# First norm of a fused two-block transformer kernel: how its sum of squares, the vector c and the constants come on chip

## What is computed

```python
c_act = jax.nn.silu(c)                       # c: (1, 1024)
mod = c_act @ w_ada[l] + b_ada[l]            # w_ada: 1024 x 6144
sh1, sc1, g1, sh2, sc2, g2 = jnp.split(mod, 6, axis=-1)
xn = modulate(rmsnorm(h, norm1_g[l]), sh1, sc1)
p = xn @ w_in[l]
...
def rmsnorm(x, g):
    y = x * lax.rsqrt(jnp.mean(x * x, axis=-1, keepdims=True) + EPS)
    return y * g
def modulate(xn, shift, scale):
    return xn * (1.0 + scale) + shift
```

## Time and profile before

| | |
|---|---|
| Median of three runs | 3202.27 us |
| The profiled execution, its own time | 3200.54 us |
| Its span in the profile | 3198.7 us (1.84 less) |
| TensorE (PE) busy | 3165.5 us, 99% of the span |
| VectorE (DVE) busy | 1867.6 us, 58% |
| ScalarE (ACT) busy | 532.1 us, 17% |
| First TensorE record | 4.00 us |
| TensorE enters the loop over k | 20.44 us |

### The profile page before, as it was taken

One profiled execution on the slowest core, in us unless ns is written; L12 is line 12 of the kernel. 1 busy time (PEld: TensorE's weight loads), 2 busy tenths in 40 slices (PEclk: granted clock), 3 DMA queues, 4 the chain that ended last, 5 costly groups with the idle time before them and its releaser, 6 DMA issues.

```text
span 3198.7 us, 36062 instructions
## 1 busy us (share of the span) xinstructions
PE 3165.5 (99%) x14174; PEld 2575.5 (81%) x14174; DVE 1867.6 (58%) x3244; ACT 532.1 (17%) x1120; POOL 240.8 (8%) x218
## 2 busy tenths in 40 slices
PE   9999999999999999999999999999999999999999
PEld 3888758888888888885488888888888854788887
DVE  6356845764347764465676664466644656766643
ACT  2111122000111000115621000110001157210001
POOL 1244410000000000003000000000000030000000
PEclk9999999999999999999999999999999999999999
DMA  5254321222222222223012222222222230122221
GB/s 239 81 183 147 143 79 53 93 79 93 85 90 82 90 89 86 89 74 119 7 66 79 93 84 91 90 79 93 86 89 89 74 119 7 61 85 93 79 84 61
DMA packets 43881, 288.28 MB, mean 90 GB/s; under 512 B 5405, under 2 KB 5405, under 8 KB 12737
## 3 DMA queue, kind: packets, MB, share of 16 engines
q1 hardware_dynamic: 39024, 271.14, 23.9%
q0 software_dynamic: 4688, 14.85, 1.4%
HBM read 281.76 MB, written 2.11 MB: 89 GB/s over the span
## 4 chain that ended last, share of the span: by engine, by line
PE 93%; DVE 4%; ACT 1%; DVEq 1%; issue 1%; DMA 0%; POOL 0%; ACTq 0%
PE ps L872 77%; PE ps L574 3%; PE ps L1283 2%; PE ps L1316 2%; PE ps L1009 2%; PE ps L1228 1%; PE ps L1297 1%; DVE arena L1953 1%; PE ps L555 1%; PE ps L899 1%; PE ps L1255 0%; PE ps L1248 0%; ACT arena L1640 0%; PE ps L956 0%; PE ps L969 0%
## 5 line engine op out<-in xcount | busy, mean ns | idle before, releaser
L872 PE MATMUL ps<-arena 128*128 128x256 f32 x5456 | 1244.9, 379 | 0.1
L872 PEld LDWEIGHTS ps<-arena 128*128 128x128 f32 x5456 | 1037.5, 190 | 140.6 <-DVE arena L2126 0.5
L872 PE MATMUL ps<-arena,ring 128*128 128x256 f32 x2768 | 646.0, 379 | 0.5 <-ACT arena L1368 0.5
L872 PEld LDWEIGHTS ps<-arena,ring 128*128 128x128 f32 x2768 | 526.0, 190 | 71.6 <-ACT arena L1368 0.9
L872 PE MATMUL ps<-xn,ring 128*128 128x256 f32 x2272 | 518.9, 379 | 5.6 <-DVE arena L1769 2.1
L872 PEld LDWEIGHTS ps<-xn,ring 128*128 128x128 f32 x2272 | 431.5, 190 | 71.4 <-issue 9.3
L1763 DVE TENSOR_TENSOR arena<-arena,ps 128x512 f32<-128x512 f32 x173 | 118.9, 687 | 545.1 <-PE ps L872 487.8
L1736 DVE TENSOR_TENSOR arena<-ring 128x512 f32<-128x512 f32 (+1 forms) x194 | 131.1, 676 | 347.9 <-PE ps L872 347.8
L872 PE MATMUL ps<-xn,arena 128*128 128x256 f32 x1264 | 302.2, 379 | 0.0
L872 PEld LDWEIGHTS ps<-xn,arena 128*128 128x128 f32 x1264 | 240.4, 190 | 32.4
L1556 ACT ACTIVATE arena<-arena 128x512 f32<-128x512 f32 x88 | 55.4, 630 | 883.6 <-DVE arena L2245 883.6
(11 more groups left out here) (327 smaller groups left out, 2510.2 us busy)
## 6 DMA issues: line engine op xcount, KB each, us to landing
ring<-in_w_up_a SPq DMA_DIRECT2D x44, 1024.0 KB, 4.8
ring<-in_w_up_b SPq DMA_DIRECT2D x44, 1024.0 KB, 4.8
ring<-in_w_ff SPq DMA_DIRECT2D x32, 1024.0 KB, 4.8
ring<-in_w_ada SPq DMA_DIRECT2D x24, 1024.0 KB, 4.9
ring<-in_w_down_a SPq DMA_DIRECT2D x16, 1024.0 KB, 4.8
ring<-in_w_down_b SPq DMA_DIRECT2D x16, 1024.0 KB, 4.8
ring<-in_w_in SPq DMA_DIRECT2D x14, 1024.0 KB, 4.8
ring<-in_w_out SPq DMA_DIRECT2D x12, 1024.0 KB, 5.6
```

The costliest lines, as they stand in the source:

```text
L872: mm = nc.tensor.matmul(out_ap, w, operand(product, quads[i]), start=at not in opened, stop=last_chunk and i == len(quads) - 1, skip_group ...
```

## The change

It has five parts.

- The constants are no longer loaded first. `ones` becomes the last of the five matrices and is written on chip by a VectorE memset; the other four are loaded ahead of the third chunk of `w_v`. TensorE's filler product reads the ones four times over in place of four constants, and there are two such products ahead of the squares, not three.
- c is loaded as one row in one partition (`c_one`). ScalarE applies Silu to that row before its squares; TensorE spreads it over all partitions by two products with a row of ones; ScalarE copies one half of the result out of PSUM and VectorE the other.
- VectorE adds squares before TensorE sees them: tiles 0 to 3 become one, and tile 7 is added to tile 5.
- TensorE multiplies four arrays by ones: the sum of tiles 0 to 3, tile 4, tile 6, and 5 with 7.
- The waits for the constants move to where another constant is first read.

```diff
-IDENT, SWAP, ONES, MEAN256, HEAD_ONES = range(5)
+IDENT, SWAP, MEAN256, HEAD_ONES, ONES = range(5)
...
+        c_one = arena[0:1, 20480:20480 + D]
...
-                nc.tensor.matmul(ps[:, bank, :], ones, consts[:, 0:4, :], start=True, stop=True)
+                nc.tensor.matmul(ps[:, bank, :], ones, consts[:, ONES:, :].to_broadcast([P, 4, P]), start=True, stop=True)
...
-            nc.sync.dma_start(consts[:, :, :], A["consts"]).then_inc(sem("in_consts"), 16)
             for half in range(2):
                 nc.sync.dma_start(h[:, 4 * half:4 * half + 4, :], A["x"][:, 4 * half:4 * half + 4, :])\
                     .then_inc(sem(f"in_x{half}"), 16)
             for name, c in ORDER_1:
+                if (name, c) == ("v", 2):
+                    nc.sync.dma_start(consts[:, 0:ONES, :], A["consts"][:, 0:ONES, :]).then_inc(sem("in_consts"), 16)
...
-            nc.gpsimd.dma_start(c_row, A["c_row"]).then_inc(sem("in_c"), 16)
+            nc.gpsimd.dma_start(c_one, A["c_row"]).then_inc(sem("in_c"), 16)
...
-            pe.wait_ge(sem("in_consts"), 16)
-
-            pe_busy(4, 3)
-            made = {"act": 0, "dve": 0}
-            for n, (t, engine) in enumerate(FIRST_SQUARES):
-                made[engine] += 1
-                pe.wait_ge(sem(f"first_sq_{engine}"), made[engine])
-                mm = nc.tensor.matmul(ps[:, 6, :], ones, first_sq[:, t, :], start=(n == 0), stop=(n == DT - 1))
-            mm.then_inc(sem("first_sum"), 1)
+            pe.wait_ge(sem("ones_made"), 1)
+            pe_busy(4, 2)
+            pe.wait_ge(sem("c_act"), 1)
+            for half in range(2):
+                nc.tensor.matmul(ps[:, half, :], ones[0:1, :], c_one[:, half * S:(half + 1) * S], start=True, stop=True)\
+                    .then_inc(sem("c_spread"), 1)
+            pe.wait_ge(sem("first_sq_added"), 1)
+            nc.tensor.matmul(ps[:, 6, :], ones, first_sq[:, 0, :], start=True, stop=False)
+            pe.wait_ge(sem("first_sq_act"), 3)
+            nc.tensor.matmul(ps[:, 6, :], ones, first_sq[:, 4, :], start=False, stop=False)
+            pe.wait_ge(sem("first_sq_dve"), 3)
+            nc.tensor.matmul(ps[:, 6, :], ones, first_sq[:, 6, :], start=False, stop=False)
+            pe.wait_ge(sem("first_sq_added"), 2)
+            nc.tensor.matmul(ps[:, 6, :], ones, first_sq[:, 5, :], start=False, stop=True).then_inc(sem("first_sum"), 1)
...
-            for t, engine in FIRST_SQUARES:
-                if engine == "act":
-                    act.wait_ge(sem(f"in_x{t // 4}"), 16)
+            act.wait_ge(sem("in_c"), 16)
+            nc.scalar.activation(c_one, c_one, ACT.Silu).then_inc(sem("c_act"), 1)
+            for half in range(2):
+                act.wait_ge(sem(f"in_x{half}"), 16)
+                for t in (4 * half, 4 * half + 1):
                     nc.scalar.activation(first_sq[:, t, :], h[:, t, :], ACT.Square).then_inc(sem("first_sq_act"), 1)
-            act.wait_ge(sem("in_c"), 16)
-            nc.scalar.activation(c_row, c_row, ACT.Silu).then_inc(sem("c_act"), 1)
+                if half == 0:
+                    act.wait_ge(sem("c_spread"), 1)
+                    nc.scalar.activation(c_row[:, 0:S], ps[:, 0, :], ACT.Copy).then_inc(sem("c_read"), 1)
...
+            nc.vector.memset(ones, 1.0).then_inc(sem("ones_made"), 1)
             nc.vector.memset(ssq[:, :], 0.0)
...
+            for half in range(2):
+                dve.wait_ge(sem(f"in_x{half}"), 16)
+                for t in (4 * half + 2, 4 * half + 3):
                     nc.vector.tensor_tensor(first_sq[:, t, :], h[:, t, :], h[:, t, :], ALU.mult)\
                         .then_inc(sem("first_sq_dve"), 1)
+                dve.drain()
+                dve.wait_ge(sem("first_sq_act"), 2 * half + 2)
+                if half == 0:
+                    nc.vector.tensor_tensor(first_sq[:, 0:2, :], first_sq[:, 0:2, :], first_sq[:, 2:4, :], ALU.add)
+                    dve.drain()
+                    nc.vector.tensor_tensor(first_sq[:, 0, :], first_sq[:, 0, :], first_sq[:, 1, :], ALU.add)\
+                        .then_inc(sem("first_sq_added"), 1)
+                    dve.wait_ge(sem("c_spread"), 2)
+                    nc.vector.tensor_copy(c_row[:, S:2 * S], ps[:, 1, :])
+                else:
+                    nc.vector.tensor_tensor(first_sq[:, 5, :], first_sq[:, 5, :], first_sq[:, 7, :], ALU.add)\
+                        .then_inc(sem("first_sq_added"), 1)
+            dve.drain()
             dve.wait_ge(sem("in_cols"), 16)
-            dve.wait_ge(sem("c_act"), 1)
+            dve.wait_ge(sem("c_read"), 1)
```

More of the change, by code:

```diff
@@ L72 @@
 FIRST_V_AT = {2: 0, 6: 1}
-FIRST_SQUARES = [(0, "act"), (2, "dve"), (1, "act"), (3, "dve"), (4, "act"), (6, "dve"), (5, "act"), (7, "dve")]
 TILES_1 = [("v", 8), ("mix", 8), ("mv", 8), ("cell", 16)]
@@ L908, in _ @@
             pe_token_product(pe, "v", 1, ST)
+            pe.wait_ge(sem("in_consts"), 16)
             pe.wait_ge(sem("x1_sums"), 4)
@@ L1809, in _ @@
             nc.vector.memset(eps_col, EPS).then_inc(sem("eps_set"), 1)
-            for t, engine in FIRST_SQUARES:
-                if engine == "dve":
-                    dve.wait_ge(sem(f"in_x{t // 4}"), 16)
+            for half in range(2):
+                dve.wait_ge(sem(f"in_x{half}"), 16)
+                for t in (4 * half + 2, 4 * half + 3):
                     nc.vector.tensor_tensor(first_sq[:, t, :], h[:, t, :], h[:, t, :], ALU.mult)\
                         .then_inc(sem("first_sq_dve"), 1)
+                dve.drain()
[11 more added lines that the diff above has]
+            dve.drain()
             dve.wait_ge(sem("in_cols"), 16)
-            dve.wait_ge(sem("c_act"), 1)
+            dve.wait_ge(sem("c_read"), 1)
             norm1 = COL1["norm1"]
@@ L2514, in lay_out @@
     A["w_ada"] = np.ascontiguousarray(f["w_ada"][0].T.reshape(48, P, D)[ADA_TILES].transpose(0, 2, 1, 3).reshape(-1, P, 2 * D))
-    A["c_row"] = np.ascontiguousarray(np.broadcast_to(f["c"].reshape(1, D), (P, D)))
+    A["c_row"] = np.ascontiguousarray(f["c"].reshape(1, D))
     A["w_v"] = np.concatenate([wide(w_in[:, D + n * S:D + (n + 1) * S]) for n in range(2)])
```

## The result

The changed kernel is slower: a median of 3206.05 us over 22 runs (3203.1 to 3208.43) where the kernel before had 3201.98 (3199.8 to 3204.32, 22 runs), a ratio of 1.0013 with a 95% interval of 1.0007 to 1.0019. I had forecast 3198.9, a gain of 3.4 us, with a range to 3203.0. It is a loss of 4.1, outside the range and inside the 0.2% in which I had put 0.92 of the chance. The profiled execution took 3203.77 us, 3.2 more than that of before; it is the second quickest of the 22 of its kernel.

The account below looks back on a forecast made before the run. TensorE, busy 99% of the span, was taken as the bound, with the loads close beside. The loop moving from 20.44 to 16.9 us gains 3.5, taken as 3.4 with the loads' limit: 3202.27 becomes 3198.9, range 3195.9 to 3203.0.

Parts of the forecast that it names:

- I take 4.2: Head: the row of c, issued at 1.33 us, lands at 4.2, between 3.2 and 5.2; TensorE waits 0.6 us.
- No row shows a 4 KB load in this head: Pricing of c's load: lacking such a row, it used small loads of the queue, 1.9 us (64 KB) and 3.9 (16 KB).
- Rival 3: Head: c late (9.8 us) holds ScalarE's squares behind Silu; loop at 22.0, 1.6 us lost, 3203.9; chance 0.08.
- TensorE, fast by then: Products on squares: fast clock from the first at 8.8 us, the fourth at 11.6 to 12.5, loop at 16.9.
- rival 1: Squares: clock stays slow, three of four products slow, loop at 19.2; gain 1.3 us, 3201.0; chance 0.20.
- the four signs of being wrong: Pitch 0.85 at 12 us; ScalarE's squares waiting for c; ada chunk 2 after 23; new TensorE wait behind 60 us.
- VectorE's four added instructions: Head: 3.3 us in all, hidden in VectorE's waiting for x half 1 and ada chunk 0.
- the cover: VectorE's waiting for x half 1 and ada chunk 0; without it the added instructions cost up to 3.3 us.
- The ones on chip: Head: a VectorE memset lets TensorE start at 1.2 us (1.0 to 1.5) in place of 4.00.
- The loads: Head: x half 1 and ada chunks come 2.0 us earlier (8.6; chunk 2 at 21.85); x half 0 at 5.4.
- From the loop on the chain is TensorE's, which carries the gain to the end.: After the loop over k starts: later steps have more slack, so the head's gain of 3.4 us reaches the end.

Follow-up runs that it names:

- ones_sums: ones_only plus VectorE's additions of squares, four products in place of eight, c still a full array: 3202.95 us, ratio 1.0005.
- wide_spread: c_sync with Silu's row in a zeroed 128-partition array and the spreading products reading all partitions: 3202.26 us, ratio 0.9999.
- thin_fill: ones_only with its three fillers ahead of the squares reduced to one partition each: 3201.72 us, ratio 0.9999.
- ones_only: Kernel before with only the ones written on chip and the other constants loaded ahead of the third w_v chunk: 3200.56 us, ratio 0.9996.
- c_sync: Changed kernel with the row of c issued by SyncE ahead of x in place of GpSimd: 3203.15 us, ratio 1.0003.
- combined4: combined with four fillers behind the squares: 3200.88 us, ratio 0.9993 to the kernel before.
- bridge: Changed kernel with four fillers ahead of the spreading in place of two, and two more behind it: 3203.97 us, ratio 1.0006.
- combined: wide_spread with one more filler ahead of the squares and VectorE's copy of c behind its last addition: 3200.02 us, once more 3199.97.
- before_again: Kernel before, unchanged, run and profiled once more: 3201.12 us, ratio 0.9997.
- before_4: Kernel before with four fillers behind the squares in place of five: 3202.13 us, ratio 0.9999.
- before_6: Kernel before with six fillers behind the squares in place of five: 3203.34 us, ratio 1.0003.
- after_pad3: Changed kernel with three one-column products behind its two fillers, where TensorE waits for c: 3203.35 us, ratio 1.0006.
- combined4_pad: combined4 with one product of one column behind its two leading fillers: 3198.50 us, ratio 0.9991 to the kernel before.
- delay2: Kernel before with seven fillers behind the squares in place of five: 3204.91 us, ratio 1.0010.
- after_again: Changed kernel, unaltered, run and profiled once more: 3205.14 us, ratio 1.0010 to the kernel before.
- the best version: The fastest kernel measured, combined4_pad: 3198.50 us, ratio 0.9991 to the kernel before.
- fill4: Changed kernel with four fillers ahead of the wait for c in place of two: 3202.77 us, ratio 1.0003.

## Why the prediction was wrong

- **"I take 4.2": the row of c.** This is the first step that failed, a wait that I had too short. I put its landing between 3.2 and 5.2, from small transfers of the same queue elsewhere in the run. It landed at 6.9 in five profiles (6.84 to 7.10). Those transfers ran beside less: 99 GB/s around the ones of 64 KB (1412 to 1416 us) and 213 around the one of 16 KB (187 to 191), against 412 from 4 to 8 us in this head. "No row shows a 4 KB load in this head" was true to the letter, but the view of the earlier trace rows has a still smaller load of the same queue in the same head, which I passed over:

```profile
gate_b<-in_gate_b POOLq DMA_DIRECT2D x1, 0.0 KB, 9.7
```

  It stood fourth in its queue, behind the array of c. Rival 3 had the mechanism, ScalarE's squares held behind Silu, with 8.5 us for its price and 1.6 us of loss at the loop; it was 5.5 us, and the loss there 1.4 to 1.45.
- **"TensorE, fast by then".** This is the second step that failed. I took the clock as lifted at 8.8 because about 5 us of work had lifted it in before. Here it was at 1.2 GHz up to 16.3 us in the first profile and from 9.0 to 15.8 in the second, for two reasons that the runs show apart: pauses (ones_sums, 3.9 us, without any product of one partition; wide_spread, 2.3 us) and spreading products of one partition, which didn't help to lift it (thin_fill against ones_only; c_sync). Pauses close in length went both ways: behind 2.17 us in combined4 the clock was still up, behind 2.27 in wide_spread it was down, and in bridge it fell behind 1.9 us and the thin products.
- **The two together.** The forecast had the loop at 16.9. With c early and the clock slow (c_sync) it starts at 19.25, where rival 1 had 19.2; the late c adds the 2.1 to 2.6 us to the 21.32 and 21.89 of the changed kernel. Rivals 1 and 3 came at once, and I had priced them only one at a time; the range ended at 3203.0, below even the 3203.9 of rival 3. Of the four signs of being wrong that I had named, three came: the pitch of 0.85 at 12 us, ScalarE's squares behind c, and the longer wait behind 60 us.
- **VectorE's four added instructions**, 3.3 us, cost what I said (1.22, 0.69, 0.69 and 0.69), but the cover was used up: they came behind c and ended at 14.5.
- **The ones on chip** went nearly as forecast: TensorE at 1.14. ones_only keeps this part and is not slower than before.
- **The loads.** The halves of x landed at 5.78 and 9.3, where I had 5.4 and 8.6: the second came 1.3 us earlier, not 2.0. In ones_only, where c is still an array, it landed at 9.37, so leaving the array out gave x next to nothing. Ada chunk 2, forecast at 21.85 in place of 23.85, landed at 22.06 in wide_spread and 22.17 in combined. It never bound the changed kernel, as the loop was later than before.
- **"From the loop on the chain is TensorE's, which carries the gain to the end."** This step failed too, by 1.1 us: from the loop to mv it is 370.9 to 371.65 us in ten profiles (before and before_again, before_4, before_6, ones_only, thin_fill, after_pad3, the two of combined, combined4_pad) and 371.95 to 372.52 in the ten others. What differs is whether GpSimd's addition meets the last of VectorE's three taps. Two edits that are no part of the change (delay2's fillers, after_pad3's products) move a kernel from one group to the other. I looked at the chain to 160 us and asked only for waits that would shrink.
- **Size.** Head 1.45 (1.39 between the second profiles) and stage 1.1 (1.0) give 2.4 to 2.6 of the 4.1 us between the medians. Between the second profiles, whose spans differ by 4.4 us, 0.7 more come between mv and 2620 us, and 1.6 at the fall of the clock there (0.3 are won back by the end): in after_again the granted clock is 0.83 from 2620 to 2630 us where it is 1.00 in before_again. Such a fall shows in twelve of the twenty profiles (nine near 2620 us, three near 1500 or 1550), among them delay2 and the best version, in none of the four of before, before_again, before_4 and before_6. The list of runs says that the changed kernel spends more time at the low clock, in the head or later: its granted clock over the whole run is 0.998 or less in 10 of the 11 executions of after_again, against 9 of the 33 of before on the same chip. It also says what that is worth: among the 22 runs of the changed kernel the four at 0.999 have a median of 3204.2 us and the three at 0.996 one of 3208.4. Why the later falls come stays open.

Why the load in the q and k stage lands about 0.6 us sooner in some kernels stays open as well: from its issue to GpSimd's start it is 7.5 to 8.0 us in the ten slower profiles and 8.2 to 8.6 in the ten others. That the placing of TensorE's program decides it is argued only: the number of products ahead of the loop is 13 in the changed kernel and 16 in before and after_pad3, but 14 (combined, combined4_pad) goes with the quick ones, and 15 and 17 lie on both sides (before_4 and before_6 quick, fill4 and bridge slow).

## What to carry to other kernels

Fewer products on TensorE aren't a gain where it waits for data anyway: ahead of the first big stage they keep its clock up, and a pause or operands of one partition there can cost more than the edit saves, so count the pauses that an edit opens, not only the work that it removes. Price a small load by transfers that run beside the same traffic, and put it ahead of the large ones if an in-order engine waits for it. A head gain of 1 us can be lost again in a stage where two other engines meet; look for the waits in the whole trace, and compare two profiles of the same kernel before a difference of 1 us is explained.

## What was not expected of the hardware

- Products whose operands have one partition run as long as full ones (3.78 us for two in c_sync, as for the two fillers ahead of them), and work of this kind didn't bring TensorE's clock up: 5.5 us of it was followed by products at 1.2 GHz (thin_fill), where 5.2 us with 128 partitions was followed by products at 2.4 (ones_only).
- A row of 4 KB took 5.5 us on GpSimd's queue beside 2 MB of x, hardly less than 126 KB in the same place (5.7, c_sync), and was used 1.5 us after its issue on SyncE's queue ahead of them (issue at 0.82, Silu at 2.35).
- VectorE's three taps over 511, 510 and 509 columns take 3.25 to 3.51 us when GpSimd's addition starts 1.1 to 1.7 us into them, and 2.40 when it starts at 1.8 or later.
